# Attention by pairs of heads with probabilities divided before the product, and head-wise state products in the recurrence

## The reference, cut to what matters

```python
s = jnp.einsum('bqhgd,bkhd->bhgqk', q_blk, k).astype(jnp.float32) * scale
p = jax.nn.softmax(s, axis=-1)
return jnp.einsum('bhgqk,bkhd->bqhgd', p.astype(v.dtype), v)
```

```python
s = s * w_t - s_kk * (kk_t * a_t) + v_t * k_t        # outer products, per head
out = s @ r_t
```

## Time and profile before

| | us |
|---|---|
| time, median of three runs | 6146.74 (6142.1 to 6148.96) |
| the profiled execution, its own time | 6147.24 |
| its span, first to last instruction | 6145.6 |
| TensorE busy | 5146.2 (84%) |
| VectorE busy | 3779.0 (61%) |
| ScalarE busy | 1319.8 (21%) |
| mean granted TensorE clock | 0.933 of full speed |

### The profile page before, as it was taken

The page is one execution under the profiler, slowest core; times in us unless marked ns, Lnnn a source line. Parts: engine busy times, 40 slices in busy tenths (PEclk is TensorE's granted clock), DMA queues, the critical chain, the costliest instruction groups (busy, mean ns, idle before and its releaser), DMA issues. The chain is left out here.

```text
span 6145.6 us, 69946 instructions
## 1 busy us (share of the span) xinstructions
PE 5146.2 (84%) x26300; PEld 2772.1 (45%) x26300; DVE 3779.0 (61%) x8463; ACT 1319.8 (21%) x3180; POOL 1494.9 (24%) x1408
## 2 busy tenths in 40 slices
PE   7989899987987777777789898999888877777777
PEld 4555588643333333333345555885433333333333
DVE  3444666526677777777544446665276777777775
ACT  1122311212222222222111222112122222222221
POOL 0100000003444444444300000000034444444443
PEclk9999999999999998999989998999999999898998
DMA  3112610528999999999831135105289999999998
GB/s 132 67 70 101 225 52 30 213 89 340 420 420 419 411 418 408 419 406 418 360 116 66 70 125 200 52 30 213 89 358 420 420 418 412 416 410 416 408 419 358
DMA packets 327770, 1664.26 MB, mean 271 GB/s; under 512 B 36200, under 2 KB 69224, under 8 KB 161792
## 3 DMA queue, kind: packets, MB, share of 16 engines
q0 software_dynamic: 193504, 1370.70, 54.3%
q1 hardware_dynamic: 133920, 289.01, 12.8%
HBM read 1585.80 MB, written 73.79 MB: 270 GB/s over the span
## 5 line engine op out<-in xcount | busy, mean ns | idle before, releaser
L2141 PE MATMUL psum<-peer_rows,peer_diagonal 128*128 128x512 f32 x5120 | 2500.9, 641 | 688.9 <-ACT peer_diagonal L2188 684.5
L2093 POOL DMA_INDIRECT peer_rows<-in_peer_rows,look_up_index x1280 | 1426.0, 1114 | 3254.2 <-PE psum L2141 1740.3
L2255 DVE CUSTOM_DVE_ANT_0 peer_rows<-peer_rows,h_rows 128x1024 f32<-128x1024 f32 x1280 | 1547.1, 1224 | 844.0 <-DMA peer_rows<-in_peer_rows,look_up_index 836.3
L2141 PEld LDWEIGHTS psum<-peer_rows,peer_diagonal 128*128 128x128 f32 x5120 | 1015.1, 204 | 2095.2 <-issue 1211.2
L2188 ACT ACTIVATE peer_diagonal<-ident_sb,peer_weight 128x128 f32<-128x128 f32 x1280 | 409.6, 390 | 703.0 <-DVE peer_weight L2227 697.8
L2182 ACT ACTIVATE peer_active<-peer_dots 128x4 f32<-128x4 f32 x324 | 66.6, 205 | 1647.3 <-DVE peer_dots L2255 1635.7
L482 PE MATMUL psum<-in_weights,h_sb 128*128 128x512 f32 (+1 forms) x800 | 309.9, 549 | 0.0
L998 PE MATMUL psum<-h_sb,rw_in_gate_weights 128*128 128x512 f32 (+1 forms) x768 | 213.7, 439 | 24.8 <-DMA rw_in_gate_weights<-in_w_gate 24.8
L975 POOL DMA_DIRECT2D rw_in_gate_weights<-in_w_gate x24 | 14.2, 594 | 864.7 <-DMA scratch_rkv_scratch<-rkv_staged 659.8
L482 PEld LDWEIGHTS psum<-in_weights,h_sb 128*128 128x128 f32 x800 | 152.0, 190 | 158.1 <-issue 154.0
L535 DVE SCALAR_TENSOR_TENSOR conv_acc<-conv_in,conv_taps,conv_acc 128x655 f32<-128x655 f32 x240 | 216.4, 902 | 8.5
(11 more groups left out here) (356 smaller groups left out, 6051.6 us busy)
## 6 DMA issues: line engine op xcount, KB each, us to landing
rw_out_mod_weights<-in_w_mod SPq DMA_DIRECT2D x16, 2048.0 KB
in_weights<-in_w_in SPq DMA_DIRECT2D x12, 2048.0 KB, 8.6
peer_rows<-in_peer_rows,look_up_index POOLq DMA_INDIRECT x1280
modulation_weights<-in_w_mod SPq DMA_DIRECT2D x8, 2048.0 KB
scratch_rw_scratch<-rw_in_direction SPq DMA_DIRECT2D x20, 768.0 KB, 6.2
wkv_own<-scratch_rw_scratch SPq DMA_DIRECT2D x20, 768.0 KB, 6.4
rw_in_gate_weights<-in_w_gate POOLq DMA_DIRECT2D x24, 512.0 KB, 5.6
scratch_rw_scratch<-rw_in_z SPq DMA_DIRECT2D x10, 1024.0 KB, 6.1
```

The costliest lines, as they stand in the source:

```text
L2093: nc.gpsimd.indirect_dma_start(rows[spot][:, :], None, t.dram["peer_rows"], bass.IndirectOffsetOnAxis(ap=index[j % 4][:, k:k + 1], axis=0) ...
L2141: last = nc.tensor.matmul(t.bank[2 * (i % 2) + c], diagonal[k % DIAGONALS][:, :], rows[spot][:, D + c * 512:D + (c + 1) * 512], start=(j = ...
L2255: v.tensor_tensor_reduce(rows[spot][:, 0:D], rows[spot][:, 0:D], h[:, :], 1.0, 0.0, ALU.mult, ALU.add, dots[b][:, k:k + 1]).then_inc(s["do ...
```

## The change

*Attention.* A round is now a pair of heads of one tile; there are 20 rounds. The two heads' scores are issued alternately, each on its half of the rows and into its own two banks. VectorE takes both maxima and biases, then for each head the reciprocal of the row sum and a product over all probabilities (up to 128x640, in place). Then come the transpositions of head 0 and head 1, each into its own bank, the fifth block into the rest of the scores' banks. The product with the values has the values stationary (128x64) and the transposed probabilities moving (128 columns), and its two heads alternate between PSUM partitions 0 to 63 and 64 to 127, so it comes out transposed. The product over 128x512 after the tile, its four transpositions and their copy from another bank are gone; one copy stays. Scores are made one round ahead, and wait until ScalarE has copied the fifth block of head 1.

*Recurrence.* The grams of both directions are issued alternately, after waiting for both. The state products are made for each head by itself, 128x64 stationary and 64 columns moving, two heads on the two halves of the PSUM partitions. `begin_inverse` is cut in two: the part from the gram alone stays at place 7, the part from `side_of` and the addition of the identity move to place 8.

The modulation's code is the same in both kernels. The diff, cut:

```diff
@@ attention, TensorE
+            def scores(r):
+                i, p = rounds[r]
+                if r:
+                    pe.wait_ge(s["scalar"], SCALAR.after(f"copied{r - 1}_1" if rounds[r - 1][0] else f"exp{r - 1}_1"))
+                for lo, hi in ((0, 512), (512, NK)) if i else ((0, P),):
+                    for e in range(2):
+                        rows, v = slice(e * HD, e * HD + HD), 0 if p // 2 == e else 1
+                        at = P if i else 0
+                        last = nc.tensor.matmul(scores_of[e][:, lo:hi], t.q_turned[rows, p, i * P:(i + 1) * P], t.keys[rows, v, at + lo:at + hi],
+                                                start=True, stop=True)
                 last.then_inc(s["tensor"], 1)
+            def turn(r, e):
+                i, _ = rounds[r]
+                pe.wait_ge(s["vector"], VECTOR.after(f"scaled{r}_{e}"))
+                for j in range(blocks_of(i)):
+                    out = turned_last[e] if j == 4 else turned_banks[e][:, j * P:(j + 1) * P]
+                    last = nc.tensor.transpose(out, probs[e][:, j * P:(j + 1) * P], t.ident[:, :])
+            def mix(r):
+                i, p = rounds[r]
+                at = p // 2 * HD
+                pe.wait_ge(s["vector"], VECTOR.after(f"copied{r}_1"))
                 if i:
+                    pe.wait_ge(s["scalar"], SCALAR.after(f"copied{r}_1"))
+                    if p == 0:
+                        pe.wait_ge(s["vector"], VECTOR.after(f"y_copied{i - 1}"))
                 for j in range(blocks_of(i)):
                     v = t.cached_v[:, at:at + HD] if j == 4 else t.qkv[:, j + (i > 0), 640 + at:640 + at + HD]
-                    last = nc.tensor.matmul(mixed_bank[:, h * HD:(h + 1) * HD], probs_turned[u % 2][:, j * P:(j + 1) * P], v,
-                                            start=(j == 0), stop=(j == blocks_of(i) - 1))
+                    for e in range(2):
+                        last = nc.tensor.matmul(mixed_bank[e * HD:e * HD + HD, p * P:(p + 1) * P], v, probs_turned[e][:, j * P:(j + 1) * P],
+                                                start=(j == 0), stop=(j == blocks_of(i) - 1))
+            scores(0)
+            for r in range(ROUNDS):
+                turn(r, 0)
+                turn(r, 1)
+                gates(r, 0)
+                if r + 1 < ROUNDS:
+                    scores(r + 1)
+                gates(r, 1)
+                mix(r)
@@ attention, VectorE
+            def divide(r, e):
+                i, p = rounds[r]
+                h, n = 2 * p + e, blocks_of(i) * P
+                dve.wait_ge(s["scalar"], SCALAR.after(f"exp{r}_{e}"))
+                nc.vector.reciprocal(inverse[:, h:h + 1], total[:, h:h + 1]).then_inc(s["vector"], 1)
+                dve.wait_ge(s["vector"], VECTOR.after(f"inverse{r}_{e}"))
+                nc.vector.tensor_scalar(probs[e][:, 0:n], probs[e][:, 0:n], inverse[:, h:h + 1], None, ALU.mult).then_inc(s["vector"], 1)
+            def prepare(r):
+                for e in range(2):
+                    bound(r, e)
+                for e in range(2):
+                    divide(r, e)
+            for r, (i, p) in enumerate(rounds):
+                copy_turned(r, 0)
+                if i and p == 0:
+                    copy_y(i - 1)
+                copy_turned(r, 1)
+                if r + 1 < ROUNDS:
+                    prepare(r + 1)
+                for at, j, g in LORA_ROUNDS:
+                    if r == at:
                         shift_lora(j, g)
@@ attention, ScalarE
+            for r, (i, p) in enumerate(rounds):
+                for e in range(2):
+                    if i:
+                        act.wait_ge(s["tensor"], TENSOR.after(f"turned{r}_{e}"))
+                        nc.scalar.copy(probs_turned[e][:, 4 * P:NK], turned_last[e]).then_inc(s["scalar"], 1)
+                    if e == 1 and r + 1 < ROUNDS:
+                        for ahead in range(2):
+                            exponentials(r + 1, ahead)
+                    if 2 * p + e in GATE_HEADS:
+                        empty_gates(i, GATE_HEADS.index(2 * p + e))
@@ recurrence, TensorE
-            def gram_of(n, k, d):
...
+            def grams_of(n, k):
+                for d in range(2):
+                    wait("turn_copied", d, 2 * n + 2)
+                    if k >= 2:
+                        wait("masked", d, 4 * n + k - 1)
+                for c in range(2):
+                    for d in range(2):
...
                 for half in range(2):
-                    p = 2 * q + half
-                    cols = slice((2 + half) * P, (3 + half) * P)
-                    mm(D[:, cols], key[i % 2][d][:, 1, p * P:(p + 1) * P], value[i % 2][d][:, p * P:(p + 1) * P], start=True, stop=False)
-                    last = mm(D[:, cols], key[i % 2][d][:, 0, p * P:(p + 1) * P], u[d][:, 2 * half:2 * half + 2, :].rearrange("p h e -> p (h e)"),
-                              start=False, stop=True)
+                    cols = slice(2 * P + half * HD, 2 * P + (half + 1) * HD)
+                    for c in (1, 0):
+                        for b in range(2):
+                            h = 2 * half + b
+                            own_cols = slice((4 * q + h) * HD, (4 * q + h + 1) * HD)
+                            last = mm(D[BLOCKS[b], cols], key[i % 2][d][:, c, own_cols], value[i % 2][d][:, own_cols] if c else u[d][:, h, :],
+                                      start=(c == 1), stop=(c == 0))
@@ recurrence, VectorE
                     if place == 7:
+                        begin_turned_inverse(n + 1)
+                    if place == 8:
                         begin_inverse(n + 1)
```

More of the change, by code:

```diff
@@ L696, in attention_stage @@
     NK = 5 * P
[L697 to L706, removed]
+    ROUNDS = TILES * PAIRS
+    rounds = [divmod(r, PAIRS) for r in range(ROUNDS)]
+    bounds = [f"{what}{{0}}_{e}" for e in range(2) for what in ("max", "bias")] + [f"{what}{{0}}_{e}" for e in range(2) for what in ("inverse", "scaled")]
+    tensor_order, vector_order, scalar_order = ["scores0"], [name.format(0) for name in bounds], ["exp0_0", "exp0_1"]
+    for r, (i, p) in enumerate(rounds):
+        ahead = r + 1 < ROUNDS
+        tensor_order += [f"turned{r}_0", f"turned{r}_1"] + [f"scores{r + 1}"] * ahead + [f"mixed{r}"]
+        vector_order += [f"copied{r}_0"] + [f"y_copied{i - 1}"] * (p == 0 and i > 0) + [f"copied{r}_1"]
+        vector_order += [name.format(r + 1) for name in bounds] * ahead
+        scalar_order += [f"copied{r}_0", f"copied{r}_1"] * (i > 0) + [f"exp{r + 1}_0", f"exp{r + 1}_1"] * ahead
+    TENSOR = Marks(*tensor_order)
     VECTOR = Marks(*vector_order, f"y_copied{TILES - 1}")
@@ L712, in sbuf @@
             return mem.enter_context(nc.sbuf_tensor("attention_" + name, [P, *shape], F32))
[L714 to L718, removed]
+        largest, bias, total, inverse = (sbuf(n, HEADS) for n in ("largest", "bias", "total", "inverse"))
+        probs = [sbuf(f"probs{e}", NK) for e in range(2)]
+        probs_turned = [sbuf(f"probs_turned{e}", NK) for e in range(2)]
         mu_lora, mu_lora_own = sbuf("mu_lora", 2, 3), sbuf("mu_lora_own", 3)
@@ L760, in _ @@
         def _(pe):
[L761 to L765, removed]
-                if i:
-                    nc.tensor.matmul(out[:, 0:512], lhs, t.keys[b:b + HD, v, P:5 * P], start=True, stop=True)
-                    last = nc.tensor.matmul(out[:, 512:640], lhs, t.keys[b:b + HD, v, 5 * P:6 * P], start=True, stop=True)
-                else:
-                    last = nc.tensor.matmul(out[:, 0:P], lhs, t.keys[b:b + HD, v, 0:P], start=True, stop=True)
-                last.then_inc(s["tensor"], 1)
@@ L1373, in between @@
                     for k in ((), (), (), (), (), (0,), (1, 2), (3,), (), ())[place]:
[L1374 to L1375 removed]
+                        grams_of(n + 1, k)
                     for d in range(2):
@@ L1394, in _ @@
             for k in range(4):
-                for d in range(2):
-                    gram_of(0, k, d)
+                grams_of(0, k)
             for d in range(2):
```

124 lines of the change are left out of this document (41 added, 83 removed).

## The result

| | before | after |
|---|---|---|
| time, median (4 runs each) | 6144.42 us | 6051.24 us (6047.54 to 6055.81) |
| ratio, 95% interval | | 0.9848 (0.9831 to 0.9865) |
| span of the profiled execution | 6145.6 | 6047.8 |
| attention stage, layer 0 and 1 | 205.8, 204.5 | 167.2, 168.4 |
| recurrence stage, layer 0 and 1 | 425.1, 424.0 | 415.8, 417.0 |

6053 us was forecast, with 68 us from attention and 26 from the recurrence. The two spans differ by 97.8 us: 74.7 of it in the attention stages, 16.3 in the recurrences, 6.8 in stages that the change doesn't touch (mostly the expert stages and the second modulation and projection, 1.6 to 4.2 each, which move by about as much from one execution to the next). A stage is counted here from its first instruction on TensorE, VectorE or ScalarE to the next stage's first.

A forecast was written before the change was run, and what follows sets the result against it. TensorE was taken to bound attention; in the recurrence TensorE and VectorE hand results back and forth. Attention's 68 us and the recurrence's 26 sum to 94, so 6147 - 94 = 6053 us, range 6022 to 6102.

The forecast's parts named there:

- Scores of a pair: Attention: two heads on opposite row halves run at once, 1.27 us for both instead of 2.54.
- values: Attention, product with the values: column halves run at once, 1.15 us a pair of heads instead of 2.32.
- ScalarE's wait: Attention, pair 1: TensorE stands 1.1 us once a latent tile while ScalarE empties head 2's gate bank before the second copy.
- latent tile: Attention: 31.7 us of TensorE's work plus waits of 1.0 and 1.1 give 33.8 us, against 42.3 before.
- Tile 0: Attention's tile 0: no gain, some 2.6 us saved and given back by the exposed first round and first latent round.
- wait for the division: Attention, pairs 2 and 3: TensorE waits 0.5 us each for divided probabilities, 1.0 us a tile.
- State products: Recurrence: 1.3 us instead of 2.0 for both directions, 0.7 a step, 7 us per layer over 10 steps.
- Split inverse: Recurrence, level 5: 1.2 us kept in five steps, zero out of steps 0, 2, 4, 6; 6 us per layer.
- Grams: Recurrence: they already overlap, so alternating the directions gives zero.
- rival of shared loads: Value and state products: column halves share the load, so their loads don't overlap; 24 us per layer, 6099 us; chance 0.15.
- rival of the longer chain: Attention rounds: division or its signals take 1.5 us longer, costing 21 us a layer, about 6095 us; chance 0.10.
- slower rival: Both attention stages held at the lower clock, growing 115 us a layer: 6283 us; chance 0.04, shared with any other loss.

The follow-up runs named there:

- recurrence alone: The kernel before the change with only the changed recurrence stage, attention as before: 6124.74 us, ratio 0.9968 to the kernel before.
- old grams: Changed kernel with the grams issued direction by direction again, as before the change: 6051.06 us.
- copies first: Changed kernel with ScalarE copying both fifth blocks of a round before it empties the gate bank of head 2: 6041.97 us.
- heads one by one: Changed kernel with a round's two heads issued one after the other in scores and value products, array halves kept: 6071.52 us.
- whole inverse: Changed kernel with all of the inverse's start joined at place 7 again: 6062.42 us.
- old products: Changed kernel with the state products 128x128 for two heads, as before the change: 6052.78 us.
- late factors: Changed kernel with VectorE's factors of a new tile, both directions, moved to place 2 of the step after the sums: 6014.46 us.
- both together: Changed kernel with ScalarE's two fifth-block copies before head 2's gate bank and VectorE's factors at place 2: 6003.57 us, ratio 0.9770 to the kernel before.
- no division: Changed kernel with the product with the reciprocal row sum covering only the first column of each head's probabilities: 6043.80 us.

## Why the prediction was right, and where its terms were off

**Attention, 34 us a layer forecast, 38.6 and 36.2 measured.** Scores of a pair were taken at 1.27 and took 1.28, values 1.15 and 1.24, the division 0.54 and 0.55, ScalarE's wait 1.1 and 1.0, and the latent tile 33.8 and 34.2. Tile 0 was taken at no gain, and took 25.9 us instead of 25.8 in layer 0 (27.1 instead of 26.3 in layer 1, with 7.9 us at the lower clock at its start instead of 5.6), from the stage's start to the first latent maximum.

That the latent tile came out within 0.4 us is in part luck. The wait for the division was oversized: in pair 2, 0.1 us instead of 0.5, and the transpositions there follow the values at once (417.91 + 1.24 = 419.15), since the gate part covers 1.9 us and not 1.72; in pair 3 leaving the division out gains 0.04. So the tile's waits are 1.15 us and not 2.1, while TensorE's work is 33.1 (34.22 less the waits) and not 31.7. Most of the latter is in the eight gate parts, which each take 0.1 to 0.3 us more than their passes stream, as the four passes from 402.52 to 404.33 above do: 1.81 for 1.72.

What was left out is on the side of the kernel before: I took its tile at 42.3, yet the four took 43.7 on average, one of them 47.90 with a stretch at the lower clock, which began 1.4 us after the wait of 1.48 us in the earlier trace rows. The runs price that stretch. From first maximum to first maximum that tile takes 48.4 us with 6.8 at the lower clock (before, layer 0), 46.7 with 3.4 (before, layer 1), and 45.1 with none, in layer 0 of the recurrence alone, whose attention code is the same and has the same wait (1.47 us). So the clock is 3.3 and 1.6 us of the gain. At full clock the four tiles give 35.3 us, 1.3 over the forecast. In the changed kernel both attention stages run at the full clock after their first 5.5 and 7.9 us.

**Recurrence, 13 us a layer forecast, 9.3 and 7.0 measured.** The mechanisms were right and the sizes not.
- State products: 0.7 us a step was the term, 0.46 is the measure. The passes were taken at the 64x64 tiles' 0.032 us, so 0.6 a direction with the switch in; they take 0.039 each, 0.62 a direction without any switch, and three changes of form cost 0.1 each on top, on the passes before or behind (0.31 to 0.32 for two that take 0.22 elsewhere): the whole of `produce` goes from 6.45 to 5.98.
- Split inverse: 1.2 us in five steps was the term, 1.06 the measure. In the steps with sums nothing, as forecast. That VectorE's chain with the factors decides there is shown by moving them: those steps lose 3.1 to 4.5 us.
- Grams: nothing, as forecast.
- The clock was kept at zero in the sum. It has two signs here. It gives back 4.9 and 3.1 us in the nine steps, which is what their 14.5 and 12.7 us hold beyond 0.46 a step and 1.06 in five of them (lower clock for 30.7 us before, 17.1 and 20.5 after). And it takes the 4.5 us at the stage's end, which is the largest part of the miss; 0.7 and 1.2 more are lost before the first right side. That the steps alone come near the 13 forecast is luck: 3 us too many in the terms, 3 to 5 from a clock that was left out.

**The sum** came out within 2 us of the median by luck in its parts: attention's 7 us too few, the recurrence's 10 too many, and the 7 us of stages that the change doesn't touch leave 4 us of the span between them. The mechanisms held, four of the sizes did not (waits, TensorE's work, state products, clock). The rival of shared loads is refuted: value passes at 0.062 in column halves, with 64 stationary columns each. The Trainium skill's rule in "TensorE: Matmul & The Clock Gate" ("Part 3: Packing small matmuls — row/col tiling"), that loads overlap only with products in another row group, does not decide here: had the loads stood alone, a pair of passes would have taken some 0.22 us (the rival's price), and it took 0.124. The rival of the longer chain, 21 us a layer, is refuted by leaving the division out, which gains 0.9. The slower rival, a lower clock for whole attention stages, didn't come: with waits of 1 us and less the granted clock stayed at full speed. Its working has a slip: a loss of 115 us a layer is 230 in all, so it would have outweighed the gain of 94 with 41% of the attention stages at the lower level, and not 80%: it lay nearer than the text says.

## What to carry to other kernels

Before counting passes, look at how they step in time: two halves of the array worked at once in places where nobody had alternated them, and alternation paid only where one half's run of passes (ten) was longer than what the queue reaches over (three). When a split makes one wait shorter, follow the other engine's order to the next handover; here the larger gain (15 us a layer) lay in moving VectorE products that nobody waited for yet out from between an addition and a mask. A stretch at the lower clock followed a wait of 2.4 us in six of ten places (1.4 to 1.6 us more) and one of 1.5 us in three of four (1.6 or 3.3 us more), so the sum of a removed wait should carry that as a term of its own, with a range down to zero. When a part is priced by leaving it out, compare tiles or steps, not whole stages, if the stages start at a changing clock.

## What the runs showed of the hardware that was not expected

**The stage's end at half the clock.** From the last right side to the next stage the changed kernel takes 26.5 us and the kernel before 22.0 (21.5 is what the changed code takes at the full clock, as in old grams). First the changed kernel's last stretch, then that of before (the columns are those of the earlier trace rows):

```profile
1059.30:1072.20 12.90, 12.16 (x285) 11.20 (x285) 5.96 (x12) 1.86 (x6) 0.00 (x0) 1.00 0.02 3
1072.20:1085.80 13.60, 10.89 (x72) 10.35 (x72) 2.30 (x8) 1.10 (x3) 0.00 (x0) 0.50 0.06 19
```

```profile
1109.30:1122.20 12.90, 12.15 (x285) 11.19 (x285) 5.95 (x12) 1.86 (x6) 0.00 (x0) 1.00 0.01 3
1122.20:1131.30 9.10, 6.39 (x56) 6.20 (x56) 2.30 (x8) 1.09 (x4) 0.00 (x0) 1.00 0.09 30
```

The first 12.9 us are the same in both, with TensorE busy for 12.2 of them. Then the clock falls to 0.50 (1.2 GHz) in the one and not in the other. It fell in both layers of the changed kernel (two profiles), of the recurrence alone and of copies first, in one layer of heads one by one, and in none of old grams, whole inverse, old products, late factors, both together and no division; the last has the same recurrence code as the changed kernel. So it is not a matter of this stage's code alone. What decides it stays open: the stretches of clock begin where they begin, and small shifts of the work against them would fit, but no run sets that shift by itself.

**Reach of TensorE's queue.** Passes for the other half of the array started over three waiting passes of the first half, both with row halves (512 moving columns, 13 ns after the first pass) and with column halves (128 moving columns, 5 ns after the seventh of ten). That the reach is counted in passes and is three in other kernels, no run here shows.
